# Gates of two of three token tiles written by GpSimd's indirect transfers instead of one-hot products, in an expert layer

## The chip, the cores and the metric

The kernel runs on one core of a Trainium2 chip. The metric is the device time of one execution in microseconds (us); less is better. A core has five engines with their own instruction streams that meet only at semaphores: TensorE (PE in the profile, PEld its weight loads), VectorE (DVE), ScalarE (ACT), GpSimd (POOL) and SyncE (SP). SP, ACT and POOL also issue DMA transfers, which run on the core's 16 DMA engines.

## The reference, cut to what matters

A two-layer trunk (a mixer, then an expert layer, twice) over 384 tokens of width 1024. The change touches the expert layer `peer` alone: each token picks, for each of 8 heads, 16 of 16,384 experts by a two-part key (two numbers of 0 to 127), and weights them by a softmax.

```python
def peer(h, w_q, sub_keys, u_tab, v_tab):        # blocks of 128 tokens
    q = (x @ w_q).reshape(n, P_HEADS, 2, P_QDIM // 2)
    s = jnp.einsum('nhjd,hjkd->nhjk', q, sub_keys)
    sv, si = lax.top_k(s, P_TOPK)                            # 16 of 128, for both halves
    cand = sv[:, :, 0, :, None] + sv[:, :, 1, None, :]       # 256 pairs
    cidx = si[:, :, 0, :, None] * P_NKEYS + si[:, :, 1, None, :]
    tv, ti = lax.top_k(cand, P_TOPK)                         # 16 of them
    eidx = jnp.take_along_axis(cidx, ti, axis=-1)
    gate = jax.nn.softmax(tv, axis=-1)
    act = jax.nn.gelu(jnp.einsum('nhkd,nd->nhk', u_tab[eidx], x))
    return jnp.einsum('nhk,nhkd->nd', gate * act, v_tab[eidx])
```

## The kernel before

The kernel does not gather experts. It computes all of them: act = gelu(u_tab h) for 16,384 experts and 384 tokens, times a gate matrix G that is zero where a token did not pick an expert, times v_tab. An expert's number is 128 i + j; G lies in device memory as `g_dram` of 24 blocks of 16 tokens, each [i, j, token], 1 MB a block (24 MB in all, 8 MB for a token tile of 128 tokens). An expert layer has these stages:

- **Scores** (L1122 to L1136): the products with the sub-keys, for three token tiles.
- **u stage**: 128 u tiles k of 128 experts (`NJ`). PE multiplies each with 24 matmuls of 384 columns (L580 to L582: the weights are split into a high and a low part, so each product has three). For every tile SP loads 512 KB into a ring of four slots, ACT makes the high part (L1251, `high`) and DVE the low part (L1597, `low`); PE accumulates in PSUM, ACT applies Gelu (L1527), and SP stores 192 KB to `act_dram` (L491).
- **v stage**: 128 v tiles, 18 matmuls of 512 columns each (L1182), with G and act read back in chunks of 8 tiles (`load_tiles`, L1498 to L1502) and multiplied on DVE.

The gates are made within the u stage, for one token tile t after another. On DVE `rank` (L2160) finds the 16 picks of each head for 128 tokens (a token is a partition, its 8 x 16 picks lie along the row), as `sel3`: i, j, and the gate. The helper `lows` puts the low parts of the coming u tiles between pieces of it. Then PE transposes `sel3` (`chosen_T`, L1144 to L1148) and `spread` (L2239) makes one-hot rows of i and j in bf16 on DVE for four tokens at a time, the second scaled by the gate in three bf16 parts. PE multiplies them (`gate_group`, L1150 to L1159, 12 matmuls of 128 columns), ACT copies the four 128 x 128 results to `gstage` (L1511), and every fourth group ACT sends one block of 1 MB (L1495). That is 32 groups a token tile.

What fixes the order is written by hand: `SPREAD_AT = [20, 54, 88]` (L112) are the u tiles from which a token tile's groups are taken, two groups ahead of each u tile, for 16 u tiles (`SPREAD_U`, `PER_U`). PE, ACT and DVE each walk the same loop, and every engine works in program order.

```python
for k in range(NJ):                          # PE, L1162 to L1170
    for t in range(NT):
        if k == SPREAD_AT[t] - 1: chosen_T(t)
        n = k - SPREAD_AT[t]
        if 0 <= n < SPREAD_U:
            for q in range(PER_U): gate_group(...)
    u_tile(k)
```

ACT's loop has the same places. At k = `NJ` - 24 = 104 and k = 108 ACT waits until all of G is stored (L1535) and issues the first two chunks of the v stage's loads. POOL issues only a few loads and stores in the whole kernel (L2354 to L2386); in an expert layer it has one, the keys, before the scores.

Of the kernel before, what the change touches and what calls it, by code (L numbers as in the profile page):

```python
# [19 lines left out]
U32 = mybir.dt.uint32  # L20
# [90 lines left out]
PARTS = 3  # L111
SPREAD_AT = [20, 54, 88]  # L112
LEAD = 2
# [15 lines left out]
def build(nc, A):  # L129
    with ExitStack() as ctx:  # L130
# [7 lines left out]
        def sem(name):  # L138
            return ctx.enter_context(nc.semaphore(name))
# [60 lines left out]
        def pair_of(ap):  # L200
# [96 lines left out]
                 area(SM + 1480, 4 * TOPK).bitcast(BF16).rearrange("p (u h) -> p u h", h=NH)]  # L297
        sel3 = area(SM + 1544, 3, 128)
        gsum = area(SM + 1928, 2, 8)
        fin_g = area(8192, D)  # L300
# [94 lines left out]
        gexp_ready = sem("gexp_ready")  # L395
        sel_ready = sem("sel_ready")
        selT_ready = sem("selT_ready")
        selT_taken = sem("selT_taken")
# [139 lines left out]
        def _(pe):  # L538
# [579 lines left out]
            def peer(layer):  # L1118
# [23 lines left out]
                def chosen_T(t):  # L1142

                    pe.wait_ge(sel_ready, NT * layer + t + 1)  # L1144
# [17 lines left out]
                for k in range(NJ):  # L1162
                    for t in range(NT):
                        if k == SPREAD_AT[t] - 1:
                            chosen_T(t)
                        n = k - SPREAD_AT[t]
                        if 0 <= n < SPREAD_U:
                            for q in range(PER_U):
                                gate_group(96 * layer + GROUPS * t + PER_U * n + q)
                    u_tile(k)  # L1170
                pe.wait_ge(g_taken, 96 * (layer + 1))
                pe.wait_ge(selT_taken, NT * (layer + 1))

# [63 lines left out]
        def _(act):  # L1237
# [248 lines left out]
            def peer(layer):  # L1486
# [17 lines left out]
                def take_group(t, n):  # L1504

                    b, q, k = (n // 4) % 2, n % 4, n % 4
                    done = 4 * NT * layer + 4 * t + n // 8
                    if q == 0 and done:
                        act.wait_ge(g_stored[b], 16 * done)
                    act.wait_ge(g_ready, 96 * layer + GROUPS * t + n + 1)  # L1510
                    act.activation(gstage[:, b, :, 4 * q:4 * q + 4].rearrange("p j t -> p t j"),  # L1511
                                   ps[:, k, :].rearrange("p (t j) -> p t j", t=4), ACT.Copy).then_inc(g_taken, 1)
                    if q == 3:
                        act.wait_ge(g_taken, 96 * layer + GROUPS * t + n + 1)
                        store_block(b, 8 * t + n // 4)

                for k in range(NJ):
                    for t in range(NT):
                        n = k - SPREAD_AT[t]
                        if 0 <= n < SPREAD_U:  # L1520
                            for q in range(PER_U):
                                take_group(t, PER_U * n + q)
                    act.wait_ge(multiplied, at + k + 1)
                    high(at + k + WB)
                    if NJ * layer + k >= ASLOTS:
                        act.wait_ge(act_stored[k % ASLOTS], 16 * ((NJ * layer + k) // ASLOTS))
                    act.activation(act_out[:, k % ASLOTS, :], ps[:, 6 + k % 2, 0:T], ACT.Gelu).then_inc(gelu_done, 1)  # L1527
                    for t in range(NT):
                        if k == SPREAD_AT[t] - 5:
                            act.wait_ge(gexp_in, NT * layer + t + 1)  # L1530
                            act.activation(tv, tv, ACT.Exp).then_inc(gexp_ready, 1)
                    if k in (NJ - 24, NJ - 20):
                        b = int(k == NJ - 20)
                        for i in range(2):
                            act.wait_ge(g_stored[i], 16 * 12 * (layer + 1))  # L1535
                        for i in range(ASLOTS):
                            act.wait_ge(act_stored[i], 16 * (NJ * layer // ASLOTS + GJ // ASLOTS * (b + 1)))
                        load_tiles(b, b)
# [48 lines left out]
        def _(dve):  # L1587
# [572 lines left out]
            def rank(layer, t, lows):  # L2160
# [66 lines left out]
                chained(dve.tensor_reduce(gsum[:, 0, :], tv, AX_X, ALU.add))  # L2227
                chained(dve.reciprocal(gsum[:, 0, :], gsum[:, 0, :]))
                tt(sel3[:, 2, :].rearrange("p (k h) -> p h k", h=NH), tv, bc(gsum[:, 0, :], 2, TOPK), ALU.mult).then_inc(sel_ready, 1)
                lows(None)  # L2230
                dve.wait_ge(selT_ready, NT * layer + t + 1)
                three = ps[:, 5, 0:3 * P].rearrange("p (w t) -> p w t", w=3)
# [3 lines left out]
                tt(selT[:, 4, :], gate_rest, selT[:, 3, :], ALU.subtract).then_inc(selT_taken, 1)  # L2236
                dve.wait_ge(selT_taken, NT * layer + t + 1)

            def spread(layer, t, lows):  # L2239
# [4 lines left out]
                def hot(n):  # L2244

                    g = 96 * layer + GROUPS * t + n
# [5 lines left out]
                if t == 0:  # L2252
                    dve.tensor_copy(iota_1, iota)
                    chained(dve.tensor_copy(iota_2, bc(iota, 2, 2)))
                hot(0)
                for n in range(GROUPS):
                    if n + 1 < GROUPS:
                        hot(n + 1)
                    g = 96 * layer + GROUPS * t + n
                    dve.wait_ge(onehot_made, g + 1)  # L2260
# [7 lines left out]
            def peer(layer):  # L2268
# [10 lines left out]
                split[1] = WB  # L2279
                lows(None)  # L2280
                dve.tensor_copy(iota_u, bc(iota[:, 0:LOOK], 2, P))
# [73 lines left out]
        def _(pool):  # L2355
# [11 lines left out]
            for d in range(2):  # L2367
                pool.wait_ge(state_ready, d + 1)
                pool.dma_start(A["out_state"][d], sfin[:, d]).then_inc(outs_done, 16)

            pool.wait_ge(hT_by_dve, 8)
# [12 lines left out]
            pool.dma_start(skT, A["keys"][1]).then_inc(keys_in, 16)  # L2384
            pool.wait_ge(selT_taken, 2 * NT)
            pool.dma_start(fin_g, A["final_norm"].partition_broadcast(P)).then_inc(fin_in, 16)  # L2386
# [98 lines left out]
```

## Time and profile before

| | |
|---|---|
| three runs, us | 3172.85, 3174.26, 3177.91 (median 3174.26) |
| the profiled execution | 3174.6 us, its span 3172.7 us |
| granted TensorE clock, mean | 0.990 |
| PE, DVE, ACT, POOL busy, us | 3059.1, 2028.2, 1147.0, 11.2 |
| DMA, mean | 186 GB/s |

The span runs from the first to the last instruction; the execution's time is 1.9 us more. A busy time counts instructions that ran, not what they were worth; "idle before" is the time in which an engine stood before an instruction, with who released it behind it. In the span the first u stage lies at about 542 to 1159 us and the second at about 2009 to 2627 us, each followed by a v stage.

### The profile page before, as it was taken

The numbers are of one execution on the slowest core, as the hardware profiler recorded it, in microseconds if no ns is written. First come the engines' busy times: TensorE is split into PE (matmuls) and PEld (weight loads), VectorE is DVE, ScalarE is ACT, GpSimd is POOL, SyncE is SP. The second block draws the span as 40 slices with busy tenths as digits, with TensorE's granted clock in tenths as the row PEclk, the third lists the DMA queues.
The fourth block names the chain that finished last, engine by engine and source line by source line (L and its number), as shares of the span: only waits on it lengthen the run. The fifth ranks groups of instructions, "written<-read, shape, count | busy, mean of one in ns | idle before, by whom it ended". The sixth has DMA issues, their size and how long they took to land.

```text
span 3172.7 us, 51951 instructions
## 1 busy us (share of the span) xinstructions
PE 3059.1 (96%) x20266; PEld 2685.3 (85%) x20266; DVE 2028.2 (64%) x4372; ACT 1147.0 (36%) x1552; POOL 11.2 (0%) x23
## 2 busy tenths in 40 slices
PE   7989899999999999999999979999999999999998
PEld 4956569999999998888888869999999998888887
DVE  3875663887878346666666475587878625666666
ACT  4611023354545332222223364354454532222222
POOL 0000000000000000000000000000000000000000
PEclk9999999999999999999999989999999999999999
DMA  6355443565665846667663313456565765766663
GB/s 233 111 182 213 163 152 105 162 222 177 212 196 195 271 155 222 226 204 236 213 204 122 107 47 126 128 184 211 182 214 185 237 223 175 241 206 216 234 205 132
DMA packets 281942, 589.16 MB, mean 186 GB/s; under 512 B 17744, under 2 KB 181712, under 8 KB 275360
## 3 DMA queue, kind: packets, MB, share of 16 engines
q1 hardware_dynamic: 140960, 428.57, 40.2%
q10 hardware_dynamic: 139008, 151.00, 14.4%
q0 software_dynamic: 1792, 7.01, 0.6%
q8 instruction: 132, 2.16, 0.3%
q14 instruction: 50, 0.41, 0.0%
HBM read 482.97 MB, written 103.55 MB: 185 GB/s over the span
## 4 chain that ended last, share of the span: by engine, by line
PE 88%; DVE 7%; DMA 2%; ACT 1%; issue 1%; ACTq 0%; SPq 0%; DVEq 0%
PE ps L1182 33%; PE ps L580 13%; PE ps L581 13%; PE ps L582 13%; PE ps L1158 4%; DVE arena L1597 4%; DMA ring<-in_ada 2%; PE ps L553 1%; PE ps L690 1%; PE ps L641 1%; DVE w_lo L1597 1%; PE ps L1131 1%; PE ps L672 1%; PE ps L757 1%; PE ps L817 0%
## 5 line engine op out<-in xcount | busy, mean ns | idle before, releaser
L1597 DVE TENSOR_TENSOR w_lo<-ring,w_hi 128x1024 fp32r<-128x1024 f32 x576 | 701.7, 1220 | 350.2 <-ACT w_hi L1251 349.3
L580 PE MATMUL ps<-hT_hi,w_hi 128*128 128x384 f32 x2576 | 874.6, 340 | 4.6 <-ACT arena L1527 4.6
L581 PE MATMUL ps<-hT_lo,w_hi 128*128 128x384 f32 x2576 | 862.4, 335 | 0.0
L582 PE MATMUL ps<-hT_hi,w_lo 128*128 128x384 f32 x2384 | 798.7, 335 | 0.0
L1251 ACT ACTIVATE w_hi<-ring 128x1024 fp32r<-128x1024 f32 x378 | 400.0, 1060 | 956.1 <-PE ps L582 801.3
L1182 PE MATMUL ps<-w_hi,ga_hi 128*128 128x512 f32 x1512 | 596.8, 395 | 0.0
L1182 PE MATMUL ps<-w_hi,ga_lo 128*128 128x512 f32 x1512 | 596.8, 395 | 0.0
L1182 PE MATMUL ps<-w_lo,ga_hi 128*128 128x512 f32 x1512 | 596.7, 395 | 0.0
L580 PEld LDWEIGHTS ps<-hT_hi,w_hi 128*128 128x128 f32 x2576 | 484.8, 188 | 8.2 <-issue 7.7
L1547 ACT ACTIVATE w_hi<-ring 128x1024 fp32r<-128x1024 f32 x224 | 238.2, 1064 | 697.8 <-PE ps L1182 651.4
L1597 DVE TENSOR_TENSOR arena<-arena 128x768 bf16<-128x768 bf16 (+10 forms) x937 | 422.3, 509 | 99.8 <-PE ps L1158 94.5
L581 PEld LDWEIGHTS ps<-hT_lo,w_hi 128*128 128x128 f32 x2576 | 485.2, 188 | 0.5
L582 PEld LDWEIGHTS ps<-hT_hi,w_lo 128*128 128x128 f32 x2384 | 448.5, 188 | 0.0
L2306 DVE CAST ga_hi<-xn 128x384 fp32r<-128x384 f32 x256 | 92.3, 361 | 423.7 <-PE ps L1182 408.5
L1182 PEld LDWEIGHTS ps<-w_hi,ga_hi 128*128 128x128 f32 x1512 | 285.0, 188 | 66.5
L1182 PEld LDWEIGHTS ps<-w_hi,ga_lo 128*128 128x128 f32 x1512 | 285.0, 188 | 66.3
L1182 PEld LDWEIGHTS ps<-w_lo,ga_hi 128*128 128x128 f32 x1512 | 285.0, 188 | 66.2
L1511 ACT ACTIVATE arena<-ps 128x512 f32<-128x512 f32 x192 | 192.4, 1105 | 1.3 <-PE ps L1158 1.0
L1158 PE MATMUL ps<-arena 128*128 128x128 bf16 x2304 | 150.8, 219 | 6.0 <-DVE arena L1597 5.6
L1158 PEld LDWEIGHTS ps<-arena 128*128 128x128 bf16 x2304 | 133.1, 97 | 23.1 <-issue 14.2
L1597 DVE TENSOR_TENSOR ga_lo<-xn,ga_hi 128x384 fp32r<-128x384 f32 x256 | 142.9, 558 | 8.9
L1597 DVE TENSOR_TENSOR xn<-arena 128x384 f32<-128x384 f32 (+2 forms) x274 | 147.2, 541 | 0.3
(313 smaller groups left out, 2131.7 us busy)
## 6 DMA issues: line engine op xcount, KB each, us to landing
ring<-in_u SPq DMA_DIRECT2D x256, 512.0 KB, 3.7
ring<-in_v SPq DMA_DIRECT2D x256, 512.0 KB, 3.3
ring<-in_ada SPq DMA_DIRECT2D x96, 512.0 KB, 4.7
act_dram<-arena SPq DMA_DIRECT2D x256, 192.0 KB, 3.9
g_dram<-arena ACTq DMA_DIRECT2D x48, 1024.0 KB, 4.2
arena<-g_dram ACTq DMA_DIRECT2D x32, 1536.0 KB, 9.5
arena<-act_dram ACTq DMA_DIRECT2D x32, 1536.0 KB, 15.4
ring<-in_mix_in SPq DMA_DIRECT2D x42, 512.0 KB, 3.3
```

The lines of the kernel that those rows point to most:

```text
L553: mm = pe.matmul(ps[g:g + 8, 6, :], silu8[:, c, b, :], w[:, 512 * cc:512 * cc + 512], start=(b == 0 and c < 4), stop=(b == 3 and c >= 4))
L580: pe.matmul(out, hi[:, c, :], hT_hi[:, c, :], start=(c == 0), stop=False)
L581: pe.matmul(out, hi[:, c, :], hT_lo[:, c, :], start=False, stop=False)
L582: mm = pe.matmul(out, lo[:, c, :], hT_hi[:, c, :], start=False, stop=(c == DC - 1))
L641: mm = pe.matmul(ps[:, 3 * nb + t, :], l_[:, c, ts], r_[:, cc, :], start=(c == 0 and m == 0), stop=(c == DC - 1 and m == 2))
L1158: mm = pe.matmul(ps[:, k, q * P:(q + 1) * P], hot_u[n % 3][:, q // 2, :, q % 2], gated_hot[n % 3][:, q // 2, w, :, q % 2], start=(w == 0), ...
L1182: mm = pe.matmul(ps[:, 2 * t + nb, :], l_[:, n % 2, ts], r_[:, cs], start=(first and q == 0), stop=False, skip_group_check=True)
L1251: act.activation(w_hi[:, g % WB, :], ring[:, g % RING, :], ACT.Copy).then_inc(hi_ready, 1)
L1511: act.activation(gstage[:, b, :, 4 * q:4 * q + 4].rearrange("p j t -> p t j"), ps[:, k, :].rearrange("p (t j) -> p t j", t=4), ACT.Copy).t ...
L1547: act.activation(w_hi[:, g % WB, :], ring[:, g % RING, :], ACT.Copy).then_inc(hi_ready, 1)
L1597: return dve.tensor_tensor(out, a, b, op)
L2306: dve.tensor_copy(ga_hi[:, k % 2, :], ga[:, k % 2, :]).then_inc(ga_high, 1)
```

## The change

Token tiles 0 and 1 no longer pass through one-hot rows (`SCATTERED = 2`); tile 2 alone does (`SPREAD = 1`). For a scattered tile DVE computes, behind `rank`, the gate and the flat position of each pick in `g_dram`. POOL first writes zeros over the 16 blocks of these tiles, in 16 transfers, and then adds the gates in with an indirect transfer for each of the 128 picks of a token, in which each of the 128 partitions sends one 4-byte number to a position of its own. Between two heads POOL waits until all transfers of the head before have landed. The groups of tile 2 move from u tile 88 to u tile 60, and the ranks of tiles 1 and 2 move up with them. ACT's two loads of G move from k = 104 and 108 to k = 116 and 120 and wait for all indirect transfers too.

```diff
-SPREAD_AT = [20, 54, 88]
+SPREAD_AT = [20, 40, 60]
+SCATTERED = 2
+SPREAD = 3 - SCATTERED
...
                 for k in range(NJ):
-                    for t in range(NT):
+                    for t in range(SCATTERED, NT):
                         if k == SPREAD_AT[t] - 1:
                             chosen_T(t)
...
-                    if k in (NJ - 24, NJ - 20):
-                        b = int(k == NJ - 20)
+                    if k in (NJ - 12, NJ - 8):
+                        b = int(k == NJ - 8)
+                        act.wait_ge(scattered, 16 * P * SCATTERED * (layer + 1))
                         for i in range(2):
-                            act.wait_ge(g_stored[i], 16 * 12 * (layer + 1))
+                            act.wait_ge(g_stored[i], 16 * 4 * SPREAD * (layer + 1))
...
+                if t < SCATTERED:
+                    tt(sc_gate[t].rearrange("p k h -> p h k"), tv, bc(gsum[:, 0, :], 2, TOPK), ALU.mult)
+                    chosen = [sel3[:, w, :].rearrange("p (k h) -> p k h", h=NH) for w in range(2)]
+                    chained(dve.scalar_tensor_tensor(chosen[1], chosen[0], float(P), chosen[1], ALU.mult, ALU.add))
+                    chained(dve.tensor_scalar(chosen[1], chosen[1], float(GBLK), float(8 * t * P * P * GBLK), ALU.mult, ALU.add))
+                    dve.tensor_scalar(sc_at[t], chosen[1], sc_tok[:, 3:4], None, ALU.add).then_inc(scatter_ready, 1)
+                    lows(None)
+                    return
...
+                dve.memset(zeros, 0.0).then_inc(zeros_ready, 1)
...
                     rank(layer, t, lows)
-                    split[1] += SPREAD_U
-                    spread(layer, t, lows)
+                    if t >= SCATTERED:
+                        split[1] += SPREAD_U
+                        spread(layer, t, lows)
...
+            def scatter_gates(layer):
+
+                pool.wait_ge(zeros_ready, layer + 1)
+                for blk in range(8 * SCATTERED):
+                    pool.dma_start(g_dram[blk].rearrange("i j t -> i (j t)").rearrange("i (r c) -> i r c", c=256), bc(zeros, 1, 8))\
+                        .then_inc(g_zeroed, 16)
+                pool.wait_ge(g_zeroed, 16 * 8 * SCATTERED * (layer + 1))
+                for t in range(SCATTERED):
+                    pool.wait_ge(scatter_ready, SCATTERED * layer + t + 1)
+                    for h in range(NH):
+                        if h:
+                            pool.wait_ge(scattered, 16 * (P * (SCATTERED * layer + t) + TOPK * h))
+                        for k in range(TOPK):
+                            pool.indirect_dma_start(g_flat, bass.IndirectOffsetOnAxis(sc_at[t][:, k, h:h + 1], 0), sc_gate[t][:, k, h:h + 1], None,
+                                                    compute_op=ALU.add).then_inc(scattered, 16)
+
             pool.wait_ge(hT_by_dve, 8)
             pool.dma_start(skT, A["keys"][0]).then_inc(keys_in, 16)
+            scatter_gates(0)
             pool.wait_ge(x_updated, 12)
```

How it moves instructions is seen best in the order of the engines. On DVE, at the end of the first `rank` (token tile 0, first layer), before:

```order
L2227 TENSOR_REDUCE arena<-arena 128x8
L2228 RECIPROCAL arena<-arena 128x8
L1597 TENSOR_TENSOR arena<-arena 128x8x16
L1597 TENSOR_TENSOR w_lo<-ring,w_hi 128x1024
L2233 CAST arena<-ps 128x384
L1597 TENSOR_TENSOR arena<-ps,arena 128x128
L2235 CAST arena<-arena 128x128
L1597 TENSOR_TENSOR arena<-arena 128x128
L2253 CAST arena<-const 128x128
L2254 CAST arena<-const 128x256
L1597 TENSOR_TENSOR arena<-arena 128x512 x4
L1597 TENSOR_TENSOR arena<-arena 128x768 x2
```

and now (line numbers of the changed kernel):

```order
L2238 TENSOR_REDUCE arena<-arena 128x8
L2239 RECIPROCAL arena<-arena 128x8
L1608 TENSOR_TENSOR arena<-arena 128x8x16
L2243 SCALAR_TENSOR_TENSOR arena<-arena 128x128
L2244 TENSOR_SCALAR arena<-arena 128x128
L2245 TENSOR_SCALAR arena<-arena 128x128
L1608 TENSOR_TENSOR w_lo<-ring,w_hi 128x1024
L2177 MAX arena<-arena 128x8 x8
```

Before, the copy of the transposed picks (L2233) and the one-hot rows (128x512 and 128x768) follow the rank; now three short instructions make the positions, and the next tile's rank (L2177) begins behind one low part. On POOL, from the load of the first layer's keys, before:

```order
L2372 DMA arena<-in_keys 128x2048
L2374 DMA arena<-in_cache_kT 128x1024
L2375 DMA arena<-in_cache_v 128x1024
L2376 DMA arena<-in_rope 128x512
L2377 DMA arena<-in_diff_lam 128x256
```

and now:

```order
L2417 DMA arena<-in_keys 128x2048
L2404 DMA g_dram<-arena 1024x1x256 x16
L2413 DMA g_dram<-arena 6291456x1 x256
L2420 DMA arena<-in_cache_kT 128x1024
L2421 DMA arena<-in_cache_v 128x1024
```

Between the keys and the second layer's caches POOL now has 16 transfers of zeros (1024 rows of 256 numbers each) and 256 indirect ones. The same stands in the second layer.

## Rows read from the trace of the kernel before

**Rows 1.** The page: busy us (share) x instructions; then the chain by line.

```profile
PE 3059.1 (96%) x20266; PEld 2685.3 (85%) x20266; DVE 2028.2 (64%) x4372; ACT 1147.0 (36%) x1552; POOL 11.2 (0%) x23
...
PE ps L1182 33%; PE ps L580 13%; PE ps L581 13%; PE ps L582 13%; PE ps L1158 4%; DVE arena L1597 4%; DMA ring<-in_ada 2%; PE ps L553 1%; PE ps L690 1%; PE ps L641 1%; DVE w_lo L1597 1%; PE ps L1131 1%; PE ps L672 1%; PE ps L757 1%; PE ps L817 0%
```

**Rows 2.** Windows: us, busy (x) of PE, PEld, DVE, ACT, POOL; clock, DMA share, GB/s.

```profile
540.00:622.00 82.00, 81.79 (x481) 81.47 (x479) 58.27 (x229) 32.74 (x45) 0.00 (x0) 1.00 0.50 153
1050.00:1080.00 30.00, 27.78 (x164) 27.49 (x162) 7.35 (x6) 10.22 (x14) 0.00 (x0) 0.94 0.87 287
542.00:1159.00 617.00, 607.64 (x4240) 597.85 (x4239) 432.44 (x1189) 285.32 (x362) 0.00 (x0) 1.00 0.61 198
2009.00:2627.00 618.00, 608.42 (x4244) 598.34 (x4243) 432.44 (x1189) 285.34 (x362) 0.53 (x1) 1.00 0.61 198
```

**Rows 3.** The chain, first u stage, tile 0's groups: start, us, what.

```profile
635.18 1.40 PE ps L1158 x24
...
713.86 1.40 PE ps L1158 x24
```

**Rows 4.** ACT in time, late in the first u stage: start, us; idle before in brackets.

```profile
1059.61 1.06 ACT L1251 ACTIVATE w_hi<-ring 128x1024 fp32r<-128x1024 f32 x1 [2.72 <-PE ps L582]
1060.83 0.41 ACTq L1500 DMA_DIRECT2D arena<-g_dram  x1
1061.27 7.07 ACTq L1502 DMA_DIRECT2D arena<-act_dram  x1
1068.46 1.06 ACT L1251 ACTIVATE w_hi<-ring 128x1024 fp32r<-128x1024 f32 x1 [7.41 <-PE ps L582]
...
1092.76 1.06 ACT L1251 ACTIVATE w_hi<-ring 128x1024 fp32r<-128x1024 f32 x1 [2.72 <-PE ps L582]
1096.92 1.06 ACT L1251 ACTIVATE w_hi<-ring 128x1024 fp32r<-128x1024 f32 x1 [2.72 <-PE ps L582]
```

**Rows 5.** PE's waits in the first u stage: total us, times, longest.

```profile
PE ps L1147 <- DVE arena L1597: 4.1, 3, 1.4
PE ps L1158 <- DVE arena L1597: 2.8, 4, 0.7
PE ps L580 <- ACT arena L1527: 2.2, 1, 2.2
```

**Rows 6.** DVE in time, around the start of the first groups.

```profile
536.14 1.35 DVE L2281 CAST arena<-const 128x2304 bf16<-128x2304 f32 x1
537.40 1.64 DVE L2166 MAX8 arena<-arena 128x8 f32<-128x128 f32 x8
548.12 1.23 DVE L1597 TENSOR_TENSOR w_lo<-ring,w_hi 128x1024 fp32r<-128x1024 f32 x1 [9.08 <-ACT w_hi L1251]
...
622.73 0.40 DVE L1597 TENSOR_TENSOR arena<-arena 128x128 f32<-128x128 f32 x1
```

**Rows 7.** POOL's transfers: us of POOL in total, mean ns of one.

```profile
L2362 POOL DMA_DIRECT2D gate_bc<-in_levels x4 | 2.7, 682 | 104.8 <-DVE arena L1597 104.8
L2372 POOL DMA_DIRECT2D arena<-in_keys x1 | 0.5, 541 | 205.0 <-DVE hT_lo L1597 205.0
L2386 POOL DMA_DIRECT2D arena<-in_final_norm x1 | 0.5, 532 | 497.4 <-DVE arena L1597 497.4
```

**Rows 8.** DMA: ACT's queue; issues (count, KB each, median us to landing).

```profile
q10 hardware_dynamic: 139008, 151.00, 14.4%
...
g_dram<-arena ACTq DMA_DIRECT2D x48, 1024.0 KB, 4.2
arena<-act_dram ACTq DMA_DIRECT2D x32, 1536.0 KB, 15.4
...
arena<-in_final_norm POOLq DMA_DIRECT2D x1, 512.0 KB, 5.0
```

**Rows 9.** POOL and DVE in time, where POOL issues its last transfer.

```profile
2429.47 0.53 POOL L2386 DMA_DIRECT2D arena<-in_final_norm  x1 [497.41 <-DVE arena L1597]
...
2428.89 4.30 DVE L1597 TENSOR_TENSOR arena<-arena 128x128 bf16<-128x128 f32 x11
```

More of the change, by code:

```diff
@@ L298, in build @@
         sel3 = area(SM + 1544, 3, 128)
+        sc_gate = [area(10496 + 256 * t, TOPK, NH) for t in range(SCATTERED)]
+        sc_at = [area(10624 + 256 * t, TOPK, NH).bitcast(U32) for t in range(SCATTERED)]
+        zeros = area(24192, 256)
+        sc_tok = area(24448, 4)
         gsum = area(SM + 1928, 2, 8)
@@ L396, in build @@
         sel_ready = sem("sel_ready")
+        zeros_ready = sem("zeros_ready")
+        g_zeroed = sem("g_zeroed")
+        scatter_ready = sem("scatter_ready")
+        scattered = sem("scattered")
         selT_ready = sem("selT_ready")
@@ L1142, in chosen_T @@
                 def chosen_T(t):
-                    pe.wait_ge(sel_ready, NT * layer + t + 1)
+                    pe.wait_ge(sel_ready, SPREAD * layer + t - SCATTERED + 1)
                     pe.wait_ge(scores_taken, 12 * (layer + 1))
@@ L1168, in peer @@
                             for q in range(PER_U):
-                                gate_group(96 * layer + GROUPS * t + PER_U * n + q)
+                                gate_group(GROUPS * (SPREAD * layer + t - SCATTERED) + PER_U * n + q)
                     u_tile(k)
-                pe.wait_ge(g_taken, 96 * (layer + 1))
-                pe.wait_ge(selT_taken, NT * (layer + 1))
+                pe.wait_ge(g_taken, GROUPS * SPREAD * (layer + 1))
+                pe.wait_ge(selT_taken, SPREAD * (layer + 1))
                 def v_tile(g, n, it=0, step=0, first=False):
@@ L1506, in take_group @@
                     b, q, k = (n // 4) % 2, n % 4, n % 4
-                    done = 4 * NT * layer + 4 * t + n // 8
+                    done = 4 * (SPREAD * layer + t - SCATTERED) + n // 8
                     if q == 0 and done:
                         act.wait_ge(g_stored[b], 16 * done)
-                    act.wait_ge(g_ready, 96 * layer + GROUPS * t + n + 1)
+                    act.wait_ge(g_ready, GROUPS * (SPREAD * layer + t - SCATTERED) + n + 1)
                     act.activation(gstage[:, b, :, 4 * q:4 * q + 4].rearrange("p j t -> p t j"),
@@ L1513, in take_group @@
                     if q == 3:
-                        act.wait_ge(g_taken, 96 * layer + GROUPS * t + n + 1)
+                        act.wait_ge(g_taken, GROUPS * (SPREAD * layer + t - SCATTERED) + n + 1)
                         store_block(b, 8 * t + n // 4)
                 for k in range(NJ):
-                    for t in range(NT):
+                    for t in range(SCATTERED, NT):
                         n = k - SPREAD_AT[t]
@@ L2228, in rank @@
                 chained(dve.reciprocal(gsum[:, 0, :], gsum[:, 0, :]))
+                if t < SCATTERED:
[6 more added lines that the diff above has]
+                    return
                 tt(sel3[:, 2, :].rearrange("p (k h) -> p h k", h=NH), tv, bc(gsum[:, 0, :], 2, TOPK), ALU.mult).then_inc(sel_ready, 1)
                 lows(None)
-                dve.wait_ge(selT_ready, NT * layer + t + 1)
+                dve.wait_ge(selT_ready, SPREAD * layer + t - SCATTERED + 1)
                 three = ps[:, 5, 0:3 * P].rearrange("p (w t) -> p w t", w=3)
@@ L2236, in rank @@
                 tt(selT[:, 4, :], gate_rest, selT[:, 3, :], ALU.subtract).then_inc(selT_taken, 1)
-                dve.wait_ge(selT_taken, NT * layer + t + 1)
+                dve.wait_ge(selT_taken, SPREAD * layer + t - SCATTERED + 1)
             def spread(layer, t, lows):
@@ L2244, in hot @@
                 def hot(n):
-                    g = 96 * layer + GROUPS * t + n
+                    g = GROUPS * (SPREAD * layer + t - SCATTERED) + n
                     if g >= 3:
@@ L2250, in hot @@
                     tt(hot_v[g % 3], bc(iota_2, 1, 2), bc(two(selT[:, 1, 4 * n:4 * n + 4]), 2, P), ALU.is_equal).then_inc(onehot_made, 1)
-                if t == 0:
+                if t == SCATTERED:
                     dve.tensor_copy(iota_1, iota)
@@ L2258, in spread @@
                         hot(n + 1)
-                    g = 96 * layer + GROUPS * t + n
+                    g = GROUPS * (SPREAD * layer + t - SCATTERED) + n
                     dve.wait_ge(onehot_made, g + 1)
@@ L2280, in peer @@
                 lows(None)
+                dve.memset(zeros, 0.0).then_inc(zeros_ready, 1)
+                number, high_part, low_part = (sc_tok[:, w:w + 1].bitcast(U32) for w in range(3))
+                chained(dve.tensor_tensor_reduce(gate_rest, ident, iota, 1.0, 0.0, ALU.mult, ALU.add, sc_tok[:, 3:4]))
+                chained(dve.tensor_copy(number, sc_tok[:, 3:4]))
+                dve.tensor_scalar(high_part, number, 4, None, ALU.logical_shift_right)
+                chained(dve.tensor_scalar(low_part, number, GBLK - 1, None, ALU.bitwise_and))
+                chained(dve.scalar_tensor_tensor(sc_tok[:, 3:4], high_part, float(P * P * GBLK), low_part, ALU.mult, ALU.add))
                 dve.tensor_copy(iota_u, bc(iota[:, 0:LOOK], 2, P))
@@ L2369, in _ @@
                 pool.dma_start(A["out_state"][d], sfin[:, d]).then_inc(outs_done, 16)
+            g_flat = g_dram.rearrange("b i j t -> (b i j t)").unsqueeze(1)
+            def scatter_gates(layer):
[12 more added lines that the diff above has]
+                                                    compute_op=ALU.add).then_inc(scattered, 16)
             pool.wait_ge(hT_by_dve, 8)
             pool.dma_start(skT, A["keys"][0]).then_inc(keys_in, 16)
+            scatter_gates(0)
             pool.wait_ge(x_updated, 12)
@@ L2384, in _ @@
             pool.dma_start(skT, A["keys"][1]).then_inc(keys_in, 16)
-            pool.wait_ge(selT_taken, 2 * NT)
+            scatter_gates(1)
+            pool.wait_ge(selT_taken, 2 * SPREAD)
             pool.dma_start(fin_g, A["final_norm"].partition_broadcast(P)).then_inc(fin_in, 16)
```

## The prediction

> **What bounds the kernel now.** The page comes first [rows 1]: PE is busy 3059.1 of 3172.7 us, and PE's lines hold nearly all of the chain. The one-hot products (L1158) have 4% of it and DVE's `arena` products 4%. So time is won here only by taking work or waits from PE. The windows [rows 2] show the two u stages, 617 and 618 us long, with PE busy about 608 us in each: they are PE's stages, alike to 1 us, and what holds for one holds for the other. POOL does nothing in them. DVE is busy 432 of 617 us and ACT 285.
>
> Then I took the pitch of a u tile from ACT's rows, because ACT makes one high part a tile: 1096.92 - 1092.76 = 4.16 us where there are no groups [rows 4]. Where there are groups, fourteen tiles lie between the first and the last row of [rows 3]: (713.86 - 635.18) / 14 = 5.62 us, of which 1.40 is the 24 matmuls of two groups. So a tile with groups costs PE 1.46 us more. Last, PE's waits [rows 5]: 4.1 + 2.8 us for DVE at the starts of three token tiles, 2.3 us each, and 2.2 us for ACT while it issues the loads of the v stage. Check: 128 x 4.16 + 48 x 1.46 + 6.9 + 2.2 = 611.7, of 617; the rest is nine transposes and the matmuls at the lower clock behind ACT's hold (0.94 in that window [rows 2]).
>
> **What is removed.** A token tile costs PE 16 x 1.46 = 23.4 us for its groups, 2.3 us of waits at its start and some 0.6 us for the transposes (an estimate from the unexplained 5 us above, of which a third or so is theirs). That is 26.3 us. Two token tiles go in each of two layers: 4 x 26.3 = 105.2 us off PE's own path, with nothing under it, since PE is the bound there. ACT loses 64 copies and 16 sends a layer, DVE its one-hot rows; both had idle time in the stage, so this is worth nothing by itself.
>
> **What is added on DVE.** Three short instructions a scattered tile (about 0.3 to 0.4 us each, like those of [rows 6]) and seven at the start of the expert layer, some 2 us. At that start DVE later stands 9.08 us for ACT [rows 6], so they are hidden. The ranks now follow each other without one-hot rows between. The first took from 537.4 to 623.1 us [rows 6], 86 us; three in a row would end by 537 + 3 x 86 = 795, and tile 2's transposes are due at u tile 59, near 542 + 59 x 4.16 = 788. The first rank includes the 9 us stand, so I expect 780 to 790 and a wait between none and 5 us beyond today's 2.3; I take 2 us a layer.
>
> **What is added on POOL.** This decides the case. First 16 transfers of zeros, 16.8 MB a layer, replace the same bytes that ACT sent as gates, but in a burst from about 538 us. The stage moves 153 GB/s there at a DMA share of 0.50, and 287 GB/s were reached at 0.87 [rows 2]. With 134 GB/s to spare the zeros need 125 us (end 663); with twice that, 63 us (end 601). The first gates are ready at 624 us, one or two us behind the first rank [rows 6], so the scatter starts between 624 and 663. POOL's issue of them: 384 rows took it 0.68 us against 0.54 for 128 [rows 7], so 1024 rows should be near 1.0 us each, 16 us in all, far below the transfer itself. I expect no loss on PE: the window at 0.87 has PE idle for ACT alone [rows 4, 5], not for weights.
>
> Then 256 indirect transfers a layer, with POOL standing at 14 places until a head has landed and ACT standing for the last. No row shows an indirect transfer. Bounds on POOL's time for one, X: not under the 0.53 us of a plain one [rows 7]; the farthest is a plain one that also stands for a whole DVE product of 1.22 us (one of 1.23 in [rows 6]), 1.76 us. It must read 128 positions and write 128 unrelated addresses, with an addition, so I take twice the plain one, 1.1 us, which lies nearest the plain row. Landing, W: 5.0 us for POOL's transfer late in the u stage, 15.4 for the slowest kind [rows 8]; I take 5, the same queue in the same stage. 256 X + 16 W = 282 + 80 = 362 us.
>
> **When it must be done.** ACT now waits at u tile 116. Before, ACT reached its loads at u tile 104 at 1060.8 us [rows 4]. Twelve tiles later and two token tiles' groups earlier is 1060.8 + 12 x 4.16 - 2 x 26.3 = 1058 us. From 624 that is 434 us, against 362: 72 us to spare, or 33 if the zeros end at 663. So the scatter is hidden, on time up to X = (434 - 80) / 256 = 1.38 us. It is covered by u tiles alone; if the cover is gone, PE stands. ACT works in order: behind its wait stand the load of G, the high parts of the coming tiles and the Gelu that frees PSUM. That is why a hold of 4.7 us (7.41 against 2.72) already cost PE 2.2 us [rows 4, 5], and a late scatter costs PE nearly all of its lateness. The loads at u tiles 116 and 120 still lie 50 and 33 us before the v stage, over the 15.4 us of the slower of them [rows 8]; ACT's 7 us hold at the issue stays as it was.
>
> **Sum.** 3174.6 - 105.2 + 2 x 2 = 3073.4 us, against the profiled execution, which is 0.3 us over the median 3174.26 of the runs. Forecast 3073.
>
> **A rule against the change.** POOL's last plain transfer was issued in 0.53 us at 2429.47, in the midst of 4.30 us of DVE's bf16 products [rows 9], and one beside no such work took 0.54 [rows 7]. So plain issue is not held by DVE. The Trainium skill (SBUF, State Buffer, section "SBUF: two separate sides") says otherwise: while VectorE runs a two-port operation, GpSimd cannot write the descriptors of its transfers and they stand. By that rule each transfer would stand for the DVE product at hand. The row does not bear it out for plain transfers, but an indirect one also reads positions from SBUF, and no row has that.
>
> **The rivals.**
> 1. *Each indirect issue stands behind a DVE instruction*, X = 1.76 us (worked out above; the skill's rule just named is this case). 256 x 1.76 + 80 = 531, end at 1155, 97 us late in each layer: 3073 + 194 = 3267, slower. It becomes slower than before from X = (434 + 51 - 80) / 256 = 1.58 us. For it: DVE is busy 70% of the stage [rows 2]. Against: [rows 9], and DVE is nearly idle after the last groups, at u tile 76. Chance 0.13.
> 2. *The DMA engines are the limit.* ACT's queue took 0.144 x 16 x 3172.7 us / 139008 packets = 53 ns a packet of 1.1 KB [rows 8]. An addition is at least a read and a write for each number: 256 packets on 16 engines, 0.84 us an engine at that price. With 0.4 of their time free (share 0.61 [rows 2]) that is 2.1 us a transfer: 538 + 80 = 618, end 1242, 184 us late, 3073 + 368 = 3441; the weights might be held too. Against it: 53 ns is mostly 1.1 KB of data, and these carry 4 bytes. Chance 0.10.
> 3. *Partly late.* X between 1.38 and 1.58, or W near 10 with zeros that end late: the end lies between 3085 and 3170. Chance 0.12.
> 4. *It cancels.* Within 0.2% (6 us, what a measurement of this kernel can tell from no change): 0.02, since only a narrow strip of X gives it.
> 5. *The expected case*, hidden, 3064 to 3085: 0.63. Below 3064 nothing leads but a longer start wait than I found.
>
> **How the numbers follow.** Faster is cases 5 and 3, 0.75; slower 1 and 2, 0.23; same 0.02. The likeliest gives 3073, with its own range 3064 to 3085. Up to 3200 the range takes in case 3 and the near edge of case 1, and leaves out about 0.19.
>
> **What would show it.** Right: PE's L1158 has 768 matmuls instead of 2304; each u stage lasts about 617 - 51 = 566 us; POOL's indirect transfers have a mean near 1.1 us, and the last lands near 986 us; ACT does not stand for POOL or for a DMA of `g_dram` at u tile 116. Wrong: a long idle of ACT before its high part near 1058 us put down to POOL or to `g_dram`, with PE idle and the granted clock low beside it (rivals 1 to 3: POOL's mean tells 1 from 2, where POOL's time would lie in its waits); or PE waiting for weights between 540 and 660 us, which would make the zeros the cost.

## The result, and the profile after

The changed kernel takes 3349.82 us (median of five runs, 3343.29 to 3362.1) against 3173.27 us before. The ratio is 1.0552, with a 95% interval of 1.0538 to 1.0566: slower by 5.5%, where 3.2% less was forecast. The profiled execution took 3362.1 us, 12 us over the median. Those 12 us lie in the first mixer, ahead of anything that the change touches, where the granted clock was lower this time. So times within the first u stage stand 12 us later in the profile of after than the forecast has them.

The page of the changed kernel, engines and costliest waits, answers to [rows 1, 2]. First busy time, then busy tenths in 40 slices and the clock, then the chain by line:

```profile
PE 2982.0 (89%) x18718; PEld 2613.1 (78%) x18718; DVE 1823.4 (54%) x3870; ACT 1027.7 (31%) x1424; POOL 939.3 (28%) x567
...
PE   7989999999998059999999989999999209999998
...
POOL 0000001377777730000000000177878770000000
PEclk8999899999999579999999989999999659999999
...
PE ps L1192 31%; POOL g_dram L2413 25%; PE ps L590 4%; PE ps L592 4%; PE ps L591 4%; DMA g_dram<-arena 4%; DMA ring<-in_ada 2%; PE ps L563 1%; DVE arena L1608 1%; PE ps L700 1%; PE ps L651 1%; DMA ring<-in_u 1%; PE ps L767 1%; PE ps L1141 1%; PE ps L682 1%
```

PE does 77 us less work than before, as forecast in kind. But PE's row has two holes, one at the end of each u stage, with the granted clock down to five and six tenths beside them, and POOL is busy right through both. A quarter of the chain is now POOL's indirect transfer (L2413), an operation that the kernel before did not have.

The windows of the changed kernel (columns as in [rows 2]) show three pieces of the first u stage, its hole, and both stages as a whole:

```profile
640.00:720.00 80.00, 80.00 (x463) 80.00 (x462) 65.72 (x252) 30.39 (x42) 64.05 (x36) 1.00 0.77 176
920.00:1000.00 80.00, 80.00 (x464) 80.00 (x463) 23.70 (x20) 28.20 (x40) 63.63 (x38) 1.00 0.78 178
1060.00:1205.00 145.00, 17.42 (x101) 17.10 (x99) 3.68 (x3) 4.31 (x6) 114.87 (x74) 0.58 0.26 20
554.00:1257.00 703.00, 561.13 (x3469) 556.46 (x3468) 328.35 (x931) 225.40 (x298) 457.05 (x268) 0.90 0.68 174
2107.00:2814.00 707.00, 559.83 (x3462) 555.43 (x3461) 328.32 (x931) 224.99 (x298) 460.47 (x268) 0.90 0.68 172
```

In the u stages PE is busy 561 and 560 us: that is the 566 us that was forecast for the whole stage, less its few waits. The stages last 703 and 707 us, where 617 and 618 stood before. The difference to the forecast is one stretch in each: in the first stage ACT stands from 1071 to 1211 us and PE from about 1077 to 1217 (the third window covers most of it), DVE with them, and POOL goes on.

ACT in order of time shows who is stood for (start, us, idle before in brackets):

```profile
1069.21 1.06 ACT L1261 ACTIVATE w_hi<-ring 128x1024 fp32r<-128x1024 f32 x1 [2.72 <-PE ps L592]
1070.18 0.47 ACT L1537 ACTIVATE arena<-ps 128x384 f32<-128x384 f32 x1
1211.08 0.41 ACTq L1510 DMA_DIRECT2D arena<-g_dram  x1
1211.52 3.77 ACTq L1512 DMA_DIRECT2D arena<-act_dram  x1
1215.42 1.06 ACT L1261 ACTIVATE w_hi<-ring 128x1024 fp32r<-128x1024 f32 x1 [144.76 <-issue]
```

ACT finishes u tile 116 at 1070.65 us, which is the forecast 1058 us plus the 12 us of the mixer. It then waits until 1211.08 us for the last indirect transfer, and issues the first load of G. PE's own waits put the price at 141 and 145 us in the two layers; this is PE's longest in each, from the list of waits (total us, times, longest):

```profile
PE ps L590 <- ACT arena L1537: 286.2, 5, 145.1
```

Before, ACT cost PE 2.2 [rows 5] and, in the second layer, 2.4 us at these places, so the new stand is 286.2 - 4.6 = 281.6 us. With the forecast gain of 105.2 us that gives 281.6 - 105.2 = 176.4 us, and the medians differ by 3349.8 - 3173.3 = 176.5 us. That they agree to 0.1 us is chance, since the interval of the ratio is some 4 us wide to each side; within it nothing else is left to explain. The two u stages by themselves give 703 + 707 - 617 - 618 = 175 us.

### The profile page after: what moved, and what is told of

Same layout as the page of the kernel before. It is cut to its first block, busy times and chain, and to the rows that moved or that the text cites. A ratio compares the mean times of both kernels' runs of the same rounds, so it can differ in the third digit from the quotient of the medians.

```text
span 3360.0 us, 48571 instructions
## 1 busy us (share of the span) xinstructions
PE 2982.0 (89%) x18718; PEld 2613.1 (78%) x18718; DVE 1823.4 (54%) x3870; ACT 1027.7 (31%) x1424; POOL 939.3 (28%) x567
## 4 chain that ended last, share of the span: by engine, by line
PE 56%; POOL 25%; DMA 7%; issue 6%; DVE 4%; ACT 1%; ACTq 0%; SPq 0%; POOLq 0%; DVEq 0%
PE ps L1192 31%; POOL g_dram L2413 25%; PE ps L590 4%; PE ps L592 4%; PE ps L591 4%; DMA g_dram<-arena 4%; DMA ring<-in_ada 2%; PE ps L563 1%; DVE arena L1608 1%; PE ps L700 1%; PE ps L651 1%; DMA ring<-in_u 1%; PE ps L767 1%; PE ps L1141 1%; PE ps L682 1%
## 5 line engine op out<-in xcount | busy, mean ns | idle before, releaser
L590 PE MATMUL ps<-hT_hi,w_hi 128*128 128x384 f32 x2576 | 869.7, 338 | 286.9 <-ACT arena L1537 286.2
L2413 POOL DMA_INDIRECT g_dram<-arena x512 | 898.1, 1754 | 284.6 <-issue 166.2
L1608 DVE TENSOR_TENSOR arena<-arena 128x768 bf16<-128x768 bf16 (+9 forms) x421 | 210.0, 544 | 36.4 <-PE ps L1168 31.4
L1537 ACT ACTIVATE arena<-ps 128x384 f32<-128x384 f32 x256 | 121.4, 474 | 16.5 <-DMA act_dram<-arena 16.2
```

The costliest lines, as they stand in the source:

```text
L590: pe.matmul(out, hi[:, c, :], hT_hi[:, c, :], start=(c == 0), stop=False)
L1608: return dve.tensor_tensor(out, a, b, op)
L2413: pool.indirect_dma_start(g_flat, bass.IndirectOffsetOnAxis(sc_at[t][:, k, h:h + 1], 0), sc_gate[t][:, k, h:h + 1], None, compute_op=ALU.a ...
```

## Why the scatter was late

POOL's groups in the changed kernel (us in total, mean ns of one, then the idle time before them and who ended it):

```profile
L2413 POOL DMA_INDIRECT g_dram<-arena x512 | 898.1, 1754 | 284.6 <-issue 166.2 <-DMA g_dram<-arena 79.9 <-DVE arena L2245 38.5
L2404 POOL DMA_DIRECT2D g_dram<-arena x32 | 29.4, 1483 | 254.9 <-DVE arena L2300 142.7 <-issue 112.1
```

The forecast had 1.1 us for an indirect transfer; the mean is 1.754. And there is a second column: 166 us of "issue", in which POOL waits for nothing that the profile shows. POOL in order of time, while all other engines stand, shows what it is:

```profile
1109.71 1.54 POOL L2413 DMA_INDIRECT g_dram<-arena  x1 [0.30 <-issue]
1111.56 1.54 POOL L2413 DMA_INDIRECT g_dram<-arena  x1 [0.30 <-issue]
1113.41 1.54 POOL L2413 DMA_INDIRECT g_dram<-arena  x1 [0.31 <-issue]
1116.67 1.54 POOL L2413 DMA_INDIRECT g_dram<-arena  x1 [1.72 <-DMA g_dram<-arena]
```

Undisturbed, an indirect transfer takes POOL 1.54 us, and 0.30 us pass before the next one: a pitch of 1.85 us. At a head's end POOL stands 1.72 us instead of 0.30. Plain transfers on POOL had no such gap: in the kernel before, two that took 0.54 and 0.53 us begin at 1699.08 and 1699.61 us. What POOL does in the 0.30 us no row shows. Beside DVE's one-hot products it looks different:

```profile
834.33 3.38 POOL L2413 DMA_INDIRECT g_dram<-arena  x1 [0.30 <-issue]
838.01 1.64 POOL L2413 DMA_INDIRECT g_dram<-arena  x1 [0.30 <-issue]
839.96 3.38 POOL L2413 DMA_INDIRECT g_dram<-arena  x1 [0.30 <-issue]
843.63 1.63 POOL L2413 DMA_INDIRECT g_dram<-arena  x1 [0.30 <-issue]
845.57 3.38 POOL L2413 DMA_INDIRECT g_dram<-arena  x1 [0.31 <-issue]
```

Here every second one takes 3.38 us, and two of them take 5.6 us, the pitch of a u tile with groups [rows 3]. DVE of the same kernel in these us:

```profile
837.47 3.31 DVE L1608 TENSOR_TENSOR arena<-arena 128x512 bf16<-128x512 bf16 x8 [1.18 <-PE ps L1168]
840.69 1.22 DVE L1608 TENSOR_TENSOR w_lo<-ring,w_hi 128x1024 fp32r<-128x1024 f32 x1
843.09 3.31 DVE L1608 TENSOR_TENSOR arena<-arena 128x512 bf16<-128x512 bf16 x8 [1.18 <-PE ps L1168]
```

The transfer from 839.96 to 843.34 begins within DVE's products, spans the whole low part of 1.22 us and ends just after the next products have begun. This places the long ones beside DVE's work. What in it holds POOL is seen where there are no groups, and DVE has one low part a u tile and nothing else (both engines, in order of time):

```profile
944.30 1.54 POOL L2413 DMA_INDIRECT g_dram<-arena  x1 [0.30 <-issue]
945.51 1.23 DVE L1608 TENSOR_TENSOR w_lo<-ring,w_hi 128x1024 fp32r<-128x1024 f32 x1 [2.93 <-ACT w_hi L1261]
946.14 2.01 POOL L2413 DMA_INDIRECT g_dram<-arena  x1 [0.30 <-issue]
```

The first transfer begins while DVE is idle and takes 1.54 us, though the low part starts before it ends. The second begins within the low part, which ends at 946.74, and takes 2.01 us: it goes on, with its full 1.54, from 946.61. The whole trace shows the same. Of the 512 transfers 270 begin while DVE is idle, and each takes 1.54 to 1.57 us, also the 105 during which DVE starts something. 127 begin within a low part, and 125 of them go on from 0.10 to 0.13 us before that low part ends. So an indirect transfer that begins within a low part stands for it, and one that begins beside an idle DVE does not stand for what starts later. The one from 839.96 fits: taken back by 1.54 from its end it goes on at 841.80, and the low part behind the products ends at 841.91. Why it also stood from the bf16 products over into that low part, where the one from 838.01 got through between two products, the rows don't say.

In the first layer the scatter runs from 639.3 to about 1211 us, 572 us. It splits so: 256 x 1.54 = 394 us of POOL's own; 241 gaps of 0.30 = 72 us; 256 x (1.747 - 1.54) = 53 us more, beside DVE's work (1.747 is this layer's mean); 14 stands at the heads, 38 us; the rest, some 14 us, is longer gaps and the last landing. The forecast was 362 us, and at 485 us the change would have been even. The first two terms alone are 466 us, and with 14 stands of 1.72 they come to 490 us: by this estimate the change would have gained nothing even without any hold by DVE.

## The experiments

Theory A: only lateness at ACT's wait costs, and the lateness is POOL's pace per indirect instruction. Theory B: the scatter slows the stage itself, through DVE, the DMA engines or the zeros. Between them stand rivals on what makes the pace.

**half_picks**, half of the indirect transfers (ACT's and POOL's wait values follow):

```diff
-                        for k in range(TOPK):
+                        for k in range(8):
                             pool.indirect_dma_start(...)
```

> Leaves out 8 of the 16 picks of each head in the scattered tiles, so 128 indirect transfers a layer instead of 256; zeros, head waits and ACT's wait stay. Theory A (only lateness at ACT's wait costs, everything else of the forecast holds): the scatter ends near 640 + 290 = 930 us, before the 1058 us at which ACT asks for it, and the time is 3073 to 3080. Theory B (indirect transfers slow the stage itself, through DVE or the DMA engines): half of that harm stays, and the time is over 3090.

Measured: 3073.06 us, ratio 0.9681 (0.9654 to 0.9708). The last transfer is issued at 958 us, 28 later than expected and still hidden. This is the forecast time of the change, 3073; that it meets it to the us is chance, as its four runs lie between 3071.5 and 3076.4 and the kernel before took 3176.9 beside them. Zeros, 128 transfers with their head stands and two token tiles without groups are all in it; all that is missing is the second half of the transfers.

**no_wait**, all transfers, but none of the other engines stands for them (POOL itself waits for them at the end of its layer):

```diff
-                        act.wait_ge(scattered, 16 * P * SCATTERED * (layer + 1))
+                        act.wait_ge(g_zeroed, 16 * 8 * SCATTERED * (layer + 1))
...
-            g_flat = g_dram.rearrange("b i j t -> (b i j t)").unsqueeze(1)
+            g_flat = g_other.rearrange("b i j t -> (b i j t)").unsqueeze(1)
```

> All 256 indirect transfers a layer go to another device tensor that nobody reads, and ACT waits for the zeros alone (so the gates of tiles 0 and 1 are missing from the result). Theory A: POOL does all its work, nobody stands for it: 3073 to 3085. Theory B: the stage is still stretched by POOL's work beside it, over 3100.

Measured: 3068.51 us, ratio 0.967 (0.9642 to 0.9699). Its window over the first u stage:

```profile
540.00:1150.00 610.00, 606.30 (x3700) 594.06 (x3699) 357.73 (x988) 240.09 (x316) 411.27 (x241) 1.00 0.82 215
```

POOL is busy 411 of 610 us and PE still 606. The scatter goes on into the v stage, to 1225 us. Theory B falls: the scatter and the zeros together take nothing from PE that can be seen, at a DMA share of 0.82 where it was 0.61 [rows 2]. Against the runs of the kernel before on the same chip, 3176.9 - 3068.5 = 108 us are won (96 to 114 by the interval), where the forecast had a gross gain of 105.2 and a net one of 101.2.

**late_load**, ACT's wait eight u tiles later:

```diff
-                    if k in (NJ - 12, NJ - 8):
-                        b = int(k == NJ - 8)
+                    if k in (NJ - 4, NJ - 2):
+                        b = int(k == NJ - 2)
```

> ACT waits for the scatter and loads G at u tiles 124 and 126 instead of 116 and 120, all else as in the change. Theory A (PE stands for exactly the lateness of the scatter): 8 tiles of 4.16 us more are covered in each layer, 3350 - 2 x 33 = 3283. Rival (the stand behind ACT's wait is set by something else, or the v stage then waits for its first chunk instead): 3310 or more.

Measured: 3294.8 us, ratio 1.0387 (1.0358 to 1.0416). 55 us are won of the 66 expected, nearer to theory A than to its rival, and 12 us over its time. The rest went in the v stages, whose first chunk of G now comes late. PE's waits in all of this kernel's execution have a row that belongs to their starts:

```profile
PE ps L1192 <- DVE ga_lo L1608: 7.0, 2, 3.7
```

In the first layer the u stage is 33.5 us shorter, which is theory A's 33, and the v stage starts some 4 us behind it and lasts 1.7 us longer (536.9 against 535.2): 28 us are left, and twice that is 56.

**plain_write**, the addition taken away:

```diff
-                            pool.indirect_dma_start(g_flat, ..., sc_gate[t][:, k, h:h + 1], None,
-                                                    compute_op=ALU.add).then_inc(scattered, 16)
+                            pool.indirect_dma_start(g_flat, ..., sc_gate[t][:, k, h:h + 1], None).then_inc(scattered, 16)
```

> The indirect transfers write instead of add (a pick that two heads share keeps one gate). Theory A (issue on POOL sets the pace, 1.54 us and 0.30 between two): POOL's mean stays within 0.1 of 1.75 us and the time within 10 us of 3350. Rival (the addition is what is slow, a read before each write): POOL's mean or the stand at the heads falls, and the time goes under 3320.

Measured: 3554.72 us, ratio 1.1225 (1.1149 to 1.13), with the four runs far apart, from 3514.49 (the profiled one) to 3583.36. The time misses both expectations. POOL's mean fell to 1.04 us, as the rival had it. POOL in order of time:

```profile
1040.07 0.95 POOL L2413 DMA_INDIRECT g_dram<-arena  x1 [0.30 <-issue]
1041.33 0.96 POOL L2413 DMA_INDIRECT g_dram<-arena  x1 [0.30 <-issue]
1042.59 0.95 POOL L2413 DMA_INDIRECT g_dram<-arena  x1 [0.30 <-issue]
```

So the addition was a part of the pace: 0.96 us without it, 1.54 with it, and the gap of 0.30 us is the same. The time rose for another reason, in the window of 640 to 800 us (columns as before):

```profile
640.00:800.00 160.00, 52.92 (x180) 42.04 (x179) 21.87 (x97) 10.05 (x14) 114.08 (x116) 0.61 0.15 37
```

The core's DMA moves 37 GB/s at a share of 0.15, with PE busy a third of the time at a granted clock of 0.61; the changed kernel moved 176 GB/s at 0.77 there. The weight stream is starved, though the DMA engines are nearly idle. Nor is it the number of packets: from 650 to 800 us POOL's queue shows 3488 for 109 transfers, 32 each, where one that adds has 142 (counted below, at rival 2).

**plain_half_rows**, plain writes of 64 positions in place of 128:

```diff
-                            pool.indirect_dma_start(g_flat, bass.IndirectOffsetOnAxis(sc_at[t][:, k, h:h + 1], 0), sc_gate[t][:, k, h:h + 1], None,
-                                                    compute_op=ALU.add)
+                            pool.indirect_dma_start(g_flat, bass.IndirectOffsetOnAxis(sc_at[t][0:64, k, h:h + 1], 0), sc_gate[t][0:64, k, h:h + 1], None)
```

> Plain writes as in plain_write, but of tokens 0 to 63 alone (the other gates of tiles 0 and 1 are left out). If the weight stream is starved by the rate at which 4-byte writes reach device memory, half of them per us starve it much less: under 3250. If it is the mixture of plain indirect transfers with the weight queue, whatever their number of positions, it stays near 3500.

Measured: 3647.53 us, ratio 1.1495 (1.1476 to 1.1514), slower still: of the two cases the second, though some 150 us over its time. Half the positions did not help, so the rate of 4-byte writes is not what starves the weights; a transfer of 64 has 32 packets like one of 128 (2432 for 76 transfers). Why plain indirect writes do it and adding ones don't stays open: the chain there names only an unknown queue.

**half_rows**, adding transfers of 64 positions, their number unchanged:

```diff
-IndirectOffsetOnAxis(sc_at[t][:, k, h:h + 1], 0), sc_gate[t][:, k, h:h + 1]
+IndirectOffsetOnAxis(sc_at[t][0:64, k, h:h + 1], 0), sc_gate[t][0:64, k, h:h + 1]
```

> Each indirect transfer carries the positions of tokens 0 to 63 alone (the gates of the other 64 tokens of tiles 0 and 1 are left out); their number stays 256 a layer. If POOL's time is per position, an undisturbed one falls from 1.54 to some 0.9 us, the scatter ends near 1010 us and the time is 3070 to 3085. If it is a price for the instruction, it stays at 1.5 and the time at 3330 to 3350.

Measured: 3282.84 us, ratio 1.0347 (1.0319 to 1.0376). POOL in order of time:

```profile
1037.44 1.40 POOL L2413 DMA_INDIRECT g_dram<-arena  x1 [0.30 <-issue]
1039.14 2.15 POOL L2413 DMA_INDIRECT g_dram<-arena  x1 [0.30 <-issue]
1041.60 1.39 POOL L2413 DMA_INDIRECT g_dram<-arena  x1 [0.31 <-issue]
```

The shortest are 1.39 us, against 1.54 for 128 positions: 64 positions are worth 0.15 us, and by a line through these two points 1.24 us is the instruction's own price (an estimate). The price is the instruction's, as the second case said, but the time is 47 us under its range: 256 x 0.15 = 38 us a layer were not allowed for. Two layers of them give 3274, and 3282.84 is 9 us over that, about the width of the interval.

**spread_late**, tile 2's groups at another time:

```diff
-SPREAD_AT = [20, 40, 60]
+SPREAD_AT = [20, 40, 88]
...
+                    if t == SCATTERED:
+                        split[1] = SPREAD_AT[t] - 18
+                        lows(None)
                     split[1] = SPREAD_AT[t] + LEAD
```

> Tile 2's rank and groups come at u tiles 70 to 104 instead of 42 to 76 (its first group at 88). Theory C (DVE's bf16 one-hot products hold POOL's indirect issue): the issues of 3.4 us, which stood at 834 to 862 us beside the groups, move to the new place of the groups, some 930 to 1010 us, and none is left between 830 and 900; the time stays within 15 us of 3350. Rival (the long issues come from where in the scatter they are, or from the DMA queue): they stay at their place in the scatter.

Measured: 3334.62 us, ratio 1.0506 (1.048 to 1.0531). POOL at the old place of the groups, then at the new one:

```profile
836.72 1.54 POOL L2416 DMA_INDIRECT g_dram<-arena  x1 [0.30 <-issue]
838.57 2.01 POOL L2416 DMA_INDIRECT g_dram<-arena  x1 [0.30 <-issue]
840.88 1.54 POOL L2416 DMA_INDIRECT g_dram<-arena  x1 [0.30 <-issue]
...
930.04 1.63 POOL L2416 DMA_INDIRECT g_dram<-arena  x1 [0.30 <-issue]
931.98 3.38 POOL L2416 DMA_INDIRECT g_dram<-arena  x1 [0.30 <-issue]
...
960.08 3.38 POOL L2416 DMA_INDIRECT g_dram<-arena  x1 [0.30 <-issue]
963.76 1.63 POOL L2416 DMA_INDIRECT g_dram<-arena  x1 [0.30 <-issue]
965.70 3.38 POOL L2416 DMA_INDIRECT g_dram<-arena  x1 [0.30 <-issue]
```

The issues of 3.38 us have moved with the groups, and none is left between 830 and 900. The groups bring work of PE and ACT along with DVE's, so this run alone would not tell which of them stretches the issues; that DVE can do it by itself the low parts above show, with no group near. The time also fell by 15 us, at the edge of what was allowed: only 6 transfers of this trace take over 3 us, where 17 did, and POOL's 256 of the first layer took 437.2 us in place of 447.3.

**zeros_only**, the kernel before with the zeros added, to a tensor that nobody reads:

```diff
+                for blk in range(16):
+                    pool.dma_start(g_other[blk].rearrange("i j t -> i (j t)").rearrange("i (r c) -> i r c", c=256), bc(zeros, 1, 8))\
+                        .then_inc(g_zeroed, 16)
```

> The kernel before, with the 16 transfers of zeros a layer (16.8 MB, to a tensor of their own) added on POOL at the same place and nothing else. Theory A (the zeros are hidden): within 0.2% of the kernel before, 3170 to 3180. Rival (the burst delays weights): 10 us a layer or more, 3195 or more.

Measured: 3181.3 us against 3174.39 us, ratio 1.0016 (1.0004 to 1.0029). Its window, beside the first of [rows 2]:

```profile
540.00:622.00 82.00, 80.30 (x477) 79.35 (x476) 55.15 (x232) 33.57 (x45) 13.70 (x16) 1.00 0.98 359
```

359 GB/s at a share of 0.98, where 153 at 0.50 stood before, and PE is busy 1.5 us less. The zeros cost some 1 to 9 us in both layers together: small, though not nothing. In the changed kernel POOL stood 112.1 us in two places, one a layer, before the last of them (the row of L2404 above), and still had them out before the first gates were ready, for which it then stood 38.5 us in both layers (the row of L2413).

**one_tile**, a single token tile scattered:

```diff
-SPREAD_AT = [20, 40, 60]
-SCATTERED = 2
+SPREAD_AT = [20, 40, 74]
+SCATTERED = 1
```

> Token tile 0 alone is scattered; tiles 1 and 2 go through one-hot rows from u tiles 40 and 74. Theory A: 128 indirect transfers from 640 us take some 290 us, done by 930, hidden; one tile's 26.3 us are won in each layer: 3174 - 53 = 3121. Rival (a fixed price of zeros and scatter that does not shrink with the number): 3140 or more.

Measured: 3116.89 us, ratio 0.9821 (0.979 to 0.9851): faster than the kernel before by 1.8% (1.5 to 2.1), within 4 us of the time that theory A gave. The last of 128 transfers is issued at 944 us.

**tile_and_half** goes to the limit that the runs so far set. Since the price is the instruction's, one transfer should take as many positions as it can. For tokens 0 to 63 of tile 1 the second eight picks of each head are copied to the upper partitions, and 64 transfers then carry half a tile:

```diff
+                    if t == 1:
+                        for a in (sc_gate[1], sc_at[1]):
+                            pool.dma_start(a[64:P, 0:8, :].rearrange("p k h -> p (k h)"), a[0:64, 8:16, :].rearrange("p k h -> p (k h)")).then_inc(packed, 16)
+                        pool.wait_ge(packed, 32 * (layer + 1))
```

> Token tile 0 is scattered as a whole, and tokens 0 to 63 of tile 1 by 64 transfers more: the second eight picks of a head are first copied to partitions 64 to 127, so that one transfer of 128 positions takes two picks of 64 tokens. One-hot groups are left for half of tile 1 and for tile 2; ACT waits at u tiles 120 and 124. 192 transfers a layer at 2.3 us from 632 us end near 1080 us, ACT asks at 1060.8 + 16 x 4.16 - 1.5 x 26.3 = 1088: hidden, and 1.5 token tiles are won a layer: 3174 - 79 = 3095. If the scatter is later than that, up to 3150.

Measured: 3101.19 us, ratio 0.9765 (0.9748 to 0.9782). It beats both kernels, and one_tile by a little: 2.35% under the kernel before, 7.4% under the change, and 6 us over the 3095 expected. PE's waits in the first u stage:

```profile
PE ps L601 <- ACT arena L1548: 1.9, 2, 1.4
PE ps L1168 <- DVE arena L1619: 1.4, 1, 1.4
```

The scatter is hidden: the last transfer is issued at 1074 us, and PE stands for ACT no longer than before.

## Why the prediction was wrong

**What held.** The gross gain: 26.3 us a token tile, 105.2 in all, was measured as 108 by no_wait; the net forecast of 3073 was met by half_picks with 3073.06. The 768 matmuls of L1168 are there. The time at which ACT asks, 1058 us, was right to a us (1070.65 with the mixer's 12). The start of the scatter was right (639.3, or 627 without the 12, in the forecast span of 624 to 663). That PE would stand for nearly all of the lateness was right: ACT's idle time was 144.8 us and PE's 139.6. The zeros hidden within a few us: right. The rank of tile 2 costs PE 0.7 us, less than feared, and the added DVE work none.

**The step that failed** is the sum "256 X + 16 W = 362 us". X was taken as 1.1 us, twice a plain transfer [rows 7]; it measured 1.54 us undisturbed and 1.754 in the mean. The gap of 0.30 us between two indirect ones was not in the sum at all: 72 us a layer. Plain transfers gave no sign of it, so a pitch should have had an upper bound above that of X. W went the other way: 38 us of stands in place of 80. The result, 572 us, is 87 us past the point of no gain, twice.

**The choice within the bounds was the error of judgement.** The bounds for X, 0.53 to 1.76, did hold the mean. The point from which the change loses, 1.58, lay in their upper part, and the value taken was the nearer to the familiar row, for an operation that no row showed. With the decision hanging on an unseen operation issued 256 times, 0.23 for the slower side was too little.

**Rival 1** had X to the digit (1.76 against 1.754), but its reason only in part, so that the digit is luck. Its time, 3267, was 83 us short: it had no gap, which is worth 2 x 72 us, and its stands were 2 x 42 us too long. The undisturbed 1.54 us has no DVE in it. DVE adds 0.2 us in the mean, and 1.8 us to single ones (3.38). The rule named there (the Trainium skill, SBUF — State Buffer, section "SBUF: two separate sides") has GpSimd's transfers stand while VectorE runs a two-port operation. The trace agrees in so far as an indirect issue stands for the low part at hand (2.01 us in place of 1.54 beside a low part), where [rows 9] shows no stand for a plain one; which of these VectorE instructions are two-port operations no run here shows. **Rival 2** falls by no_wait: 256 transfers beside the weights cost PE nothing that the run could tell. The priced packet was wrong in kind as well. From 1060 to 1200 us, nearly all of it without weights, queue 0 (POOL's, 4-byte packets) shows 10080 packets at a 19.5% share of 16 x 140 us for 71 transfers, from this answer of the changed kernel's DMA view:

```profile
q0 software_dynamic: 10080, 0.04, 19.5%
```

That is 43 ns a packet, near the 53 assumed, but 142 packets a transfer and not 256: 0.4 us of each engine for 1.85 us of POOL. POOL is the bound and the DMA engines are not.

## What to carry to other kernels

Work moved to an idle engine is free only while its elapsed time, gaps between instructions included, is under the cover; here 256 indirect transfers at a pitch of 1.85 us, at least, had 434 us. When the decision hangs on an operation that the trace doesn't show, put its threshold next to its bounds and give the losing side the share of the bounds that it holds. And when the price is the instruction's and not the position's, take fewer and fuller instructions, or move only what fits: one token tile turned 5.5% slower into 1.8% faster, and one and a half tiles into 2.35%.

## What the runs showed of the hardware that was not expected

An indirect transfer of 128 4-byte additions takes POOL 1.54 us, one of 64 takes 1.39, a plain one of 128 takes 0.96, and each is followed by 0.30 us. One that begins within one of VectorE's low parts stands for it, to within 0.13 us of its end, and one that begins beside an idle VectorE does not, whatever starts later. Indirect additions beside a weight stream cost it nothing that PE felt. Plain indirect writes, which are quicker to issue, brought the same stream to 37 GB/s with the DMA engines at a share of 0.15, and halving their positions made it no better. The cause of that was not found.
